# First attention's scores as two single-pass products of split queries and keys, started one chunk later

## The reference, cut to what matters

```python
q, k, v = heads(aq, 8), heads(ak, 8), heads(av, 8)
c = cumsum(log_sigmoid(af + b_forget))            # per head and token
for block i of 128 queries:
    s = q_i @ k.T * 64 ** -0.5 + c_i[:, None] - c[None, :]
    p = softmax(where(kpos <= qpos, s, -1e30))
    out_i = p @ v
```

## Time and profile before

| | |
|---|---|
| median of 3 runs | 1932.91 us (1932.16 to 1934.13) |
| the profiled execution | 1933.07 us, span 1931.3 us |
| PE busy, PEld busy | 1911.7 us (99%), 1587.9 us (82%) |
| DVE, ACT, POOL busy | 1068.6 us (55%), 832.6 us (43%), 107.4 us (6%) |
| mean granted TensorE clock | 0.997 of full |
| stage A, layer 1 and 2 | from 94.03 and from 1049.86 us |

### The profile page before, as it was taken

How to read it: one execution, slowest core, us unless ns; L and a number is a source line. 1 busy time by engine, 2 the same in 40 slices (tenths; PEclk the granted TensorE clock), 3 DMA queues, 4 the chain that set the end, 5 groups by cost and what they waited for, 6 DMA issues and landing times.

```text
span 1931.3 us, 25981 instructions
## 1 busy us (share of the span) xinstructions
PE 1911.7 (99%) x9273; PEld 1587.9 (82%) x9273; DVE 1068.6 (55%) x1914; ACT 832.6 (43%) x1429; POOL 107.4 (6%) x86
## 2 busy tenths in 40 slices
PE   8999999999999999999999999999999999999998
PEld 7888888888888888888898888888888888888886
DVE  3644555544577767425755445554455777773266
ACT  3254545543354444214433545455433544442252
POOL 1000000111001111000000000000110011110000
PEclk9999999999999999999999999999999999999999
DMA  5411243114413333332243112431244233333322
GB/s 165 99 45 44 74 101 88 55 55 150 145 44 98 98 98 98 100 114 93 85 137 88 44 48 73 101 86 55 66 153 120 66 98 98 93 97 116 97 88 77
DMA packets 255332, 176.17 MB, mean 91 GB/s; under 512 B 51045, under 2 KB 238721, under 8 KB 254977
## 3 DMA queue, kind: packets, MB, share of 16 engines
q1 hardware_dynamic: 254856, 174.65, 30.6%
q10 hardware_dynamic: 376, 0.21, 0.1%
HBM read 169.39 MB, written 4.36 MB: 90 GB/s over the span
## 4 chain that ended last, share of the span: by engine, by line
PE 98%; DVE 1%; issue 0%; DMA 0%; ACT 0%; SPq 0%; ACTq 0%; DVEq 0%
PE psum L638 85%; PE psum L813 4%; PE psum L845 3%; PE psum L828 2%; PE psum L684 1%; PE psum L841 1%; PE psum L853 1%; PE psum L825 0%; DMA xt<-in_x_dram 0%; DVE xt L1534 0%; PE psum L665 0%; PE psum L650 0%; DVE rtmp L1505 0%; DVE xnl L1445 0%; PE psum L672 0%
## 5 line engine op out<-in xcount | busy, mean ns | idle before, releaser
L638 PE MATMUL psum<-xnh,wh 128*128 128x512 f32 x1392 | 559.2, 402 | 0.6 <-DVE ub L1784 0.4
L1431 DVE TENSOR_TENSOR wl<-raw,wh 128x1024 fp32r<-128x1024 f32 (+1 forms) x272 | 355.6, 1308 | 349.6 <-ACT wh L1100 349.0
L638 PE MATMUL psum<-xnh,wl 128*128 128x512 f32 x1392 | 543.5, 390 | 0.0
L638 PE MATMUL psum<-xnl,wh 128*128 128x512 f32 x1392 | 542.4, 390 | 0.0
L1100 ACT ACTIVATE wh<-raw 128x1024 fp32r<-128x1024 f32 (+1 forms) x272 | 283.8, 1044 | 394.9 <-PE psum L638 389.1
L638 PEld LDWEIGHTS psum<-xnh,wl 128*128 128x128 f32 x1392 | 261.2, 188 | 56.0
L638 PEld LDWEIGHTS psum<-xnh,wh 128*128 128x128 f32 x1392 | 261.9, 188 | 52.2 <-issue 4.4
L638 PEld LDWEIGHTS psum<-xnl,wh 128*128 128x128 f32 x1392 | 262.0, 188 | 48.0
L1159 ACT ACTIVATE PT<-psum 128x128 f32<-128x128 f32 (+4 forms) x192 | 73.1, 381 | 152.1 <-PE psum L828 113.5
L1593 DVE CUSTOM_DVE_ANT_0 Sp<-psum,ptok 128x128 f32<-128x128 f32 (+3 forms) x128 | 62.5, 490 | 110.7 <-issue 57.0
L638 PE MATMUL psum<-wh,fh 128*128 128x512 f32 x288 | 112.0, 389 | 0.0
(11 more groups left out here) (268 smaller groups left out, 2942.4 us busy)
## 6 DMA issues: line engine op xcount, KB each, us to landing
raw<-in_w_up_dram SPq DMA_DIRECT2D x88, 512.0 KB, 3.7
raw<-in_w_gate_dram SPq DMA_DIRECT2D x48, 512.0 KB, 3.7
raw<-in_w_down_dram SPq DMA_DIRECT2D x44, 512.0 KB, 3.5
raw<-in_w_in_dram SPq DMA_DIRECT2D x30, 512.0 KB, 3.6
raw<-in_w_out_dram SPq DMA_DIRECT2D x16, 512.0 KB, 3.5
raw<-in_w_ple_gate_dram SPq DMA_DIRECT2D x16, 512.0 KB, 3.8
raw<-in_w_in_dram SPq DMA_DIRECT2D x16, 260.0 KB, 2.8
raw<-in_w_in_dram SPq DMA_DIRECT2D x16, 256.0 KB, 3.4
```

Of the source, the lines that this page charges most:

```text
L638: ins = pe.matmul(out, left, right, start=start and n == 0, stop=stop and n == 2)
L1431: dve.tensor_tensor(low[:, 0:n], raw[(L * NCH + c) % RAW][:, 0:n], hi[:, 0:n].bitcast(F32), ALU.subtract).then_inc(w_lo.sem, 1)
```

## The change

Scaled keys and queries go first to the scratch tiles `th`. ACT makes rounded copies of them (high parts), DVE the differences (low parts). The contraction of the scores is laid over 128 rows: `qA` holds a head's high part in one half of the partitions and its low part in the other, `kA` the keys' high part in both halves. A second product has 66 rows: `qA1` holds the queries' high part and two rows of ones, `kAl` the keys' low part and the forget row split in two (`nf_split`). Each score is the sum of these two float32r products, over at least 256 columns. ACT does four copies of 64 x 512 a chunk, DVE one scaling of 128 x 512 and two subtractions of 64 x 512. SP issues 16 small DMAs for the split forget row at the same position. Stage A starts at chunk 17 and takes five chunks; stage C stays at chunk 22.

```diff
-ST_A = ST_KA + 8
+ST_A = ST_KA + 9
-STAGES = [(0, ST_A, ST_A + 6), (1, ST_A + 6, ST_LAT)]
+STAGES = [(0, ST_A, ST_A + 5), (1, ST_A + 5, ST_LAT)]
...
-                if c == ST_A + 1:
-                    wait(nf_ready.sem, nf_ready.at(L, 1))
+                if c == ST_A:
+                    wait(nf_lo.sem, nf_lo.at(L, 1))
                     for h in range(H):
-                        sp.dma_start(kA[HD:HD + 1, h, :], kf[32 + h:33 + h, :]).then_inc(nf_placed.sem, 16)
+                        for j in range(2):
+                            sp.dma_start(kAl[HD + j:HD + j + 1, h, :].bitcast(F32), nf_split[j][h:h + 1, :].bitcast(F32)
+                                         ).then_inc(nf_placed.sem, 16)
...
                 if a == 0 and i == 0:
-                    pe.wait_ge(g_empty.sem, g_empty.at(L, G_BASE[ST_KA + 4] + h // 2 + 1))
+                    pe.wait_ge(qk_twice.sem, qk_twice.at(L, 4 + h // 2 + 1))
+                    pe.wait_ge(qk_lo.sem, qk_lo.at(L, 4 + h // 2 + 1))
...
                 if a == 0:
-                    q, k = qA[0:HD + 1, h, P * i:P * i + P], kA[0:HD + 1, h, 0:nk(i)]
+                    n0 = max(nk(i), 2 * P)
+                    pe.matmul(o[:, 0:n0], qA[:, h, P * i:P * i + P], kA[:, h, 0:n0], start=True, stop=False)
+                    pe.matmul(o[:, 0:n0], qA1[0:HD + 2, h, P * i:P * i + P], kAl[0:HD + 2, h, 0:n0],
+                              start=False, stop=True).then_inc(s_full.sem, 1)
...
+            elif kind in ("kA", "qA"):
+                act.wait_ge(g_empty.sem, g_empty.at(L, g + 1))
+                twice = (kA, kA) if kind == "kA" else (qA, qA1)
+                for h in range(2):
+                    ins = act.activation(twice[0][HD * h:HD * h + HD, 2 * m + h, :], th[m % 2][HD * h:HD * h + HD, :],
+                                         ACT.Copy)
+                ins.then_inc(qk_hi.sem, 1)
+                for h in range(2):
+                    other = HD * (1 - h) if kind == "kA" else 0
+                    ins = act.activation(twice[1][other:other + HD, 2 * m + h, :], th[m % 2][HD * h:HD * h + HD, :],
+                                         ACT.Copy)
+                ins.then_inc(qk_twice.sem, 1)
...
+        def apart_lo(L, c):
+
+            kind, m = CHUNKS[c]
+            n = m if kind == "kA" else 4 + m
+            if kind == "kA" and m == 0 and L > 0:
+                dve.wait_ge(x_spilled.sem, 16 * L)
+            dve.wait_ge(qk_hi.sem, qk_hi.at(L, n + 1))
+            for h in range(2):
+                own, other = slice(HD * h, HD * h + HD), slice(HD * (1 - h), HD * (1 - h) + HD)
+                hi_ = (kA if kind == "kA" else qA)[own, 2 * m + h, :]
+                out = kAl[0:HD, 2 * m + h, :] if kind == "kA" else qA[other, 2 * m + h, :]
+                ins = dve.tensor_tensor(out, th[m % 2][own, :], hi_.bitcast(F32), ALU.subtract)
+            ins.then_inc(qk_lo.sem, 1)
...
                 if kind == "kA":
-                    heads_apart(L, b, kA, m, rb, g_empty)
+                    dve.tensor_tensor(th[m % 2][:, :], b[:, :], rb[:, :], ALU.mult).then_inc(g_empty.sem, 1)
                 elif kind == "qA":
-                    for r in range(2):
-                        ins = dve.scalar_tensor_tensor(out=qA[0:HD, 2 * m + r, :], in0=b[HD * r:HD * r + HD, :],
-                                                       scalar=ASCALE, in1=rb[HD * r:HD * r + HD, :],
-                                                       op0=ALU.mult, op1=ALU.mult)
-                    ins.then_inc(g_empty.sem, 1)
+                    dve.scalar_tensor_tensor(out=th[m % 2][:, :], in0=b[:, :], scalar=ASCALE, in1=rb[:, :],
+                                             op0=ALU.mult, op1=ALU.mult).then_inc(g_empty.sem, 1)
...
             if kind != "ukn":
                 lo(L, c + 1)
+            if last in ("kA", "qA"):
+                apart_lo(L, c - 1)
...
-            pool.memset(qA[HD:HD + 1, :, :], 1.0).then_inc(ones_set.sem, 1)
+            pool.memset(qA1[HD:HD + 2, :, :].bitcast(F32), 1.0).then_inc(ones_set.sem, 1)
```

More of the change, by code:

```diff
@@ L259, in trunk_kernel @@
     nf_ready = Tally(sem("nf_ready"), 1)
-    nf_placed = Tally(sem("nf_placed"), 16 * H)
+    nf_hi = Tally(sem("nf_hi"), 1)
+    nf_lo = Tally(sem("nf_lo"), 1)
+    nf_placed = Tally(sem("nf_placed"), 16 * 2 * H)
+    qk_hi = Tally(sem("qk_hi"), KT)
+    qk_twice = Tally(sem("qk_twice"), KT)
+    qk_lo = Tally(sem("qk_lo"), KT)
     ones_set = Tally(sem("ones_set"), 1)
@@ L350, in here @@
         return nc.alloc_sbuf_tensor_at(name, shape, dt, offset=base + int(kb * 1024))
-    qA = here("qA", 0, [P, H, T])
-    kA = here("kA", 24, [P, H, T])
+    qA = here("qA", 0, [P, H, T], F32R)
+    kA = here("kA", 24, [P, H, T], F32R)
+    qA1 = here("qA1", 74, [P, H, T], F32R)
+    kAl = here("kAl", 116, [P, H, T], F32R)
     vA = here("vA", 16, [P, TB, 512])
@@ L376, in trunk_kernel @@
     PT = [here(f"PT{i}", 100 + 2 * i, [P, T]) for i in range(2)]
+    nf_split = [Pr[0][32:40, :].bitcast(F32R), PT[1][32:40, :].bitcast(F32R)]
     th = [here(f"th{i}", 104 + 2 * i, [P, T]) for i in range(2)]
@@ L787, in attention @@
             if s == 0:
-                if a < 2:
-                    pe.wait_ge(g_empty.sem, g_empty.at(L, G_BASE[ST_KA + 4 if a == 0 else ST_A + 5]))
+                if a == 1:
+                    pe.wait_ge(g_empty.sem, g_empty.at(L, G_BASE[ST_A + 4]))
                 if a == 0:
-                    pe.wait_ge(nf_placed.sem, nf_placed.at(L, 16 * H))
+                    pe.wait_ge(nf_placed.sem, nf_placed.at(L, 16 * 2 * H))
                     pe.wait_ge(ones_set.sem, ones_set.at(L, 1))
@@ L812, in attention @@
                     q, k = qB[0:NOPE + ROPE, h, P * i:P * i + P], kB[0:NOPE + ROPE, h, 0:nk(i)]
-                pe.matmul(o[:, 0:windowed(s)[2] if a == 1 else nk(i)], q, k, start=True, stop=True
-                          ).then_inc(s_full.sem, 1)
+                if a > 0:
+                    pe.matmul(o[:, 0:windowed(s)[2] if a == 1 else nk(i)], q, k, start=True, stop=True
+                              ).then_inc(s_full.sem, 1)
             if 2 <= s <= STEPS + 1:
@@ L1332, in _ @@
             for c in range(ST_KA + 3, ST_A):
+                if c == ST_KA + 5:
+                    act.wait_ge(nf_ready.sem, nf_ready.at(L, 1))
+                    act.activation(nf_split[0], kf[32:40, :], ACT.Copy).then_inc(nf_hi.sem, 1)
                 if c == ST_KA + 7:
@@ L1863, in _ @@
                     gates_out(L)
+                if c == ST_KA + 5:
+                    dve.wait_ge(nf_hi.sem, nf_hi.at(L, 1))
+                    dve.tensor_tensor(nf_split[1], kf[32:40, :], nf_split[0].bitcast(F32), ALU.subtract
+                                      ).then_inc(nf_lo.sem, 1)
                 if c == ST_KA + 6:
```

## The result

The changed kernel takes 1920.38 us, median of 4 runs (1920.09 to 1921.44), against 1932.81 (4 runs, 1932.16 to 1934.13) for the kernel before on the same chip: ratio 0.9933 as estimated from all runs, interval 0.9920 to 0.9945 (the quotient of the two medians is 0.9936). The forecast was 1921.0. The profiled execution took 1920.52 us.

A forecast was written before the change was run, and what follows sets the result against it. PE was taken to work almost without pause, so its shorter turns less new waits set the time: 1933.07 - 13.8 + 2.1 - 0.2 = 1921.2, by the median 1921.0 us; range 1917.5 to 1927.0.

The forecast's parts named there:

- The scores: Attention scores on PE: split passes take 1.30 us a head instead of 2.16, saving 13.8 us in all.
- The float32 rate for narrow passes: Rival for the scores: 256-column single passes take 0.22 us, 6.2 us more, 1927 in all; chance 0.05.
- loads that add to the passes: Rival for the scores: loads of the stationary operands are not hidden, 14 us more, 1935; chance 0.02.
- The lower bound: Scores' 256-column pass: at least 0.11 us, half a 128-column float32 score; the saving would be 14.6 us.
- The waits: Denser stage, starts of the first two chunks: PE waits 1.0 us a layer more, 2.1 in all, bounds 0 and 7.8.
- The first: First chunk of the stage: the first value product waits 0.10 us for ACT's copy of block 0.
- the second: First chunk of the stage: the scores of step 4 wait 0.39 us for row maximum 2, behind the weight split.
- the third: First chunk of the stage: transposes 2 wait 0.27 us for the exponential.
- the fourth of 0.08: First chunk of the stage: value product 1 waits another 0.08 us.
- The rival with waits in each chunk: Dense stage: waits come at every chunk start, 7.8 us instead of 2.1, 1926.7 in all; chance 0.13.
- Chunk 13: Start of chunk 13 on PE: a delay of 0.11 us behind the weight split goes, 0.2 us in all.
- the last rival: Slower: every step waits for DVE and ACT; no gain from 0.16 us a step, 1938 at 0.25; chance 0.04.

The follow-up runs named there:

- narrow: The changed kernel with the first query block's scores over their own 128 columns instead of 256; 1920.20 us, ratio 0.9934.
- lo_later: The changed kernel with DVE doing the steps of three places, not two, before the weight split in stage A; 1917.49 us, again 1918.99.
- copy_first: The changed kernel with DVE's weight split one step later and ACT's first block copy ahead of its weight copy in stage A's first chunk; 1918.25 us.
- dense_alone: The kernel before, float32 scores kept, with stage A moved to chunk 17 over five chunks; 1933.19 us, ratio 1.0003.
- six_chunks: The changed kernel with split scores kept but stage A back at chunk 16 over six chunks; 1927.55 us, ratio 0.9974.
- six_spread: Split scores, stage A from chunk 16 over six chunks, last query chunk's copies put behind steps 3 and 4, subtractions behind step 4; 1921.06 us.
- more_dmas: The changed kernel with 32 small DMAs of the forget row instead of 16, the added ones to an unread tile; 1929.82 us, one run.

## Why the prediction was right

**The scores.** Forecast 1.30 us a head, measured 1.29. The extrapolated 256 columns (0.123) came at 0.117 for the first product and 0.122 for the second, by the median of 32. The float32 rate for narrow passes is excluded by these rows, and loads that add to the passes by all of them: 256 columns with a new stationary operand in 0.12 us leave no room for 0.11 on top. The Trainium skill's page "TensorE: Matmul & The Clock Gate", Part 3 ("What overlaps and what doesn't"), has loads overlap a running matmul only in another row group; the traces do not agree with that line, whereas "The mechanism" in the same Part 3 also lets a load go ahead into a background weight buffer, and no run here tells whether that happens. The lower bound, 0.11 for any narrow pass, was about right for a reason that the prediction only touched: a pass of 128 columns can start its follower after 0.06 (narrow), but with what it costs the instructions behind, a pair of them is only 0.04 shorter than a pair of 256, which makes 0.10 a pass.

**The waits.** Forecast 1.0 a layer more than before, measured 1.1, and placed right: before the value product of the first chunk, the scores of step 4 and the transposes behind them, and at step 12, which needs the row maximum of step 10; none from the third chunk on. Single terms were less good. The first was 0.24, not 0.10; the second 0.39 as forecast; the third 0.20 for 0.27; the fourth of 0.08 was not there, but PE's restart behind a wait costs 0.05 to 0.1 each time (value product to next pass 0.25 instead of 0.14), which no term had. Two sizes that were too small also cancelled in part: the first chunk loses 1.08, not 0.84, and the kernel before lost 0.45 there, not 0.28. The cause is shown, not only placed: lo_later took the waits for DVE away by order alone, copy_first the one for ACT. dense_alone adds what the forecast did not separate: five chunks alone cost 0.66 a layer, the shorter scores the other 0.45.

**Beside the chunks.** Chunk 13 gave back 0.2 a layer, 0.4 in all, where the forecast had 0.11 a layer and 0.2 in all: PE's second pass there had also been late by 0.08. ACT's four copies and SP's 16 DMAs lie in cover, with margins of 0.6 and 6.7 us where I had 0.8 and about 5; both were used up by experiment, and both then cost time. The rival with waits in each chunk falls with the timeline, since waits stop after the second.

**What it had not seen.** The prediction took the later start as given and costed only its density. That the last queries' copies must not stand right ahead of the first exponential, six_chunks showed and six_spread explained. The sum was right without it since the changed kernel has that chunk.

**Slips in the sums.** Twice 0.56 + 0.45 is 2.0, not 2.1. The exponential of the third step ends at 5.33 + 0.50 = 5.83, not 5.85. In the last rival the thresholds of 0.16 and 0.21 us a step count from 1921 and the price at 0.25 from 1919.1. From the prediction's own 0.208 the projections with a load on top would need 0.315, not 0.320. None moves the forecast by more than 0.1 us.

**Agreement to 0.6 us is partly luck.** The stretches give -12.1 where the prediction had -11.9 (-14.0, +2.2 and -0.4 by terms, for -13.8, +2.1 and -0.2), but the start of the program moves by up to 2.4 us between executions, so a median of four runs could have come a microsecond to either side.

## What to carry to other kernels

When PE has no idle time, a change is worth what its turns get shorter, read start to start, less the waits at the few points where PE catches up with engines that work in a fixed order; look for a long instruction of theirs (a weight rounding or split) that idles or runs ahead of a short one which PE needs. A batch of copies that ACT owes should not stand ahead of a stage's first exponential and its table load: begin the stage a chunk later, or put the copies behind the first steps. And compare versions over the stretch that the change touches: its length repeated here to 0.01 us, while whole times of one version came 1.5 us apart.

## What the hardware showed that I had not expected

- After PE had idled 2.4 us (six_chunks) the granted clock fell to its lower level for about 3.4 us, and likewise after 3.5 us (more_dmas); after waits of 0.2 to 0.5 us (the changed kernel's stage A) it stayed at 1.00. So 2.4 us of idle time cost over 4.
- Of two float32r passes of 128 columns (narrow) the second starts 0.06 us behind the first, and what follows 0.11 behind the second, be it transposes or a pass of 512 columns. The weight loads start 0.11 apart, the instruction behind the pair takes 0.02 to 0.05 longer, and a step gains 0.04 over 256 columns.
- A table load of 1.28 us stands in ACT's order like any instruction. It cost nothing in the changed kernel, where ACT was then idle until 99.79, and added its full length ahead of the first exponential in six_chunks.
